# Shared values computed token by token, a shorter tail after attention, and two low parts moved to VectorE, in a two-layer RWKV and differential-attention trunk

## The reference, cut to what matters

```
x = x + (p @ w_up) * sigmoid(rmsnorm(x, g) @ w_gate)          # end of the first layer
h = rmsnorm(x, kv_norm_g)
k = rmsnorm_per_64(h @ w_k);  v = h @ w_v                      # v: 8 heads of 128
q = rmsnorm_per_64(rmsnorm(x, norm_g[1, 0]) @ w_q)
attn = softmax(q1 k1 + bias) - lam * softmax(q2 k2 + bias)     # per head, causal
o = rmsnorm_per_128(attn @ v) * (1 - lambda_init)
x = x + o @ w_o
x = x + squared_relu_mlp(rmsnorm(x, ...)) ; x = x + gated embedding
```

## Time and profile before

| what | us |
|---|---|
| three runs: median (lowest to highest) | 1518.47 (1514.57 to 1519.07) |
| the profiled execution: its own time | 1517.53 |
| its span in the profile | 1515.7 |
| TensorE busy, share of the span | 1451.2, 96% |
| DVE, ACT, POOL busy | 697.9, 583.2, 543.8 |

### The profile page before, as it was taken

The page is one execution under the profiler, slowest core; times in us unless marked ns, Lnnn a source line. Parts: engine busy times, 40 slices in busy tenths (PEclk is TensorE's granted clock), DMA queues, the critical chain, the costliest instruction groups (busy, mean ns, idle before and its releaser), DMA issues.

```text
span 1515.7 us, 23392 instructions
## 1 busy us (share of the span) xinstructions
PE 1451.2 (96%) x9087; PEld 1159.8 (77%) x9087; DVE 697.9 (46%) x1134; ACT 583.2 (38%) x922; POOL 543.8 (36%) x301
## 2 busy tenths in 40 slices
PE   6999998889999999999998999898999999999998
PEld 5767877756888888888876778565888888888877
DVE  7799977557443101331258323576453201331153
ACT  6785436454323111322244324385332211322252
POOL 3130013222443444343534334343334443444332
PEclk9999999999999999999999999899999999999999
DMA  6212100311323332323231522100132323222231
GB/s 192 83 56 84 56 1 10 114 31 39 100 85 109 111 97 83 111 83 111 87 108 65 167 84 83 56 2 29 56 106 88 112 97 111 84 95 99 95 99 56
DMA packets 121950, 126.45 MB, mean 83 GB/s; under 512 B 6268, under 2 KB 118652, under 8 KB 121864
## 3 DMA queue, kind: packets, MB, share of 16 engines
q1 hardware_dynamic: 121168, 123.99, 25.2%
q0 software_dynamic: 320, 0.66, 0.2%
q10 hardware_dynamic: 376, 0.61, 0.2%
HBM read 123.12 MB, written 2.12 MB: 83 GB/s over the span
## 4 chain that ended last, share of the span: by engine, by line
PE 84%; DVE 7%; ACT 4%; issue 3%; POOL 1%; ACTq 0%; DVEq 0%; POOLq 0%
PE pb L592 24%; PE pb L593 24%; PE pb L594 24%; ACT whi L1400 1%; PE pb L722 1%; PE pb L1306 1%; PE pb L1331 1%; PE pb L1315 1%; PE pb L797 1%; DVE xl L2363 1%; DVE Lg L2525 1%; DVE tmp L2447 1%; DVE At L2536 1%; POOL wlo L498 0%; PE pb L949 0%
## 5 line engine op out<-in xcount | busy, mean ns | idle before, releaser
L495 POOL TENSOR_TENSOR wlo<-wraw,whi 128x1024 fp32r<-128x1024 f32 x99 | 237.9, 2403 | 712.4 <-ACT whi L1400 698.7
L592 PE MATMUL pb<-xh,whi 128*128 128x512 f32 x1152 | 453.7, 394 | 6.2 <-DVE xl L2363 2.1
L593 PE MATMUL pb<-xl,whi 128*128 128x512 f32 x1152 | 448.6, 389 | 0.0
L594 PE MATMUL pb<-xh,wlo 128*128 128x512 f32 x1152 | 448.4, 389 | 0.0
L1400 ACT ACTIVATE whi<-wraw 128x2048 fp32r<-128x2048 f32 x108 | 206.2, 1909 | 225.1 <-PE pb L594 225.1
L592 PEld LDWEIGHTS pb<-xh,whi 128*128 128x128 f32 x1152 | 216.2, 188 | 67.3 <-issue 19.8
L594 PEld LDWEIGHTS pb<-xh,wlo 128*128 128x128 f32 x1152 | 216.3, 188 | 45.4
L593 PEld LDWEIGHTS pb<-xl,whi 128*128 128x128 f32 x1152 | 216.3, 188 | 44.4 <-issue 1.0
L498 POOL TENSOR_TENSOR wlo<-wraw,whi 128x1024 fp32r<-128x1024 f32 x99 | 243.9, 2464 | 0.0
L592 PE MATMUL pb<-hid_h,whi 128*128 128x512 f32 x512 | 199.3, 389 | 0.0
L594 PE MATMUL pb<-hid_h,wlo 128*128 128x512 f32 x512 | 199.2, 389 | 0.0
(11 more groups left out here) (306 smaller groups left out, 1685.7 us busy)
## 6 DMA issues: line engine op xcount, KB each, us to landing
wraw<-in_mlp_w_dram SPq DMA_DIRECT2D x128, 512.0 KB, 4.3
wraw<-in_rwkv_w_rkvo_dram SPq DMA_DIRECT2D x32, 512.0 KB, 4.4
wraw<-in_ple_w_gate_dram SPq DMA_DIRECT2D x16, 512.0 KB, 4.3
xtok<-in_x_dram SPq DMA_DIRECT2D x8, 512.0 KB, 6.3
wraw<-in_w_k_shared_dram SPq DMA_DIRECT2D x8, 512.0 KB, 4.0
wraw<-in_w_v_shared_dram SPq DMA_DIRECT2D x8, 512.0 KB, 4.3
wraw<-in_diff_w_q_dram SPq DMA_DIRECT2D x8, 512.0 KB, 3.9
wraw<-in_diff_w_o_dram SPq DMA_DIRECT2D x8, 512.0 KB, 4.3
```

Of the source, the lines that this page charges most:

```text
L495: pool.tensor_tensor(wlo[:, par, front], wraw[:, par, front], whi[:, par, front].bitcast(F32), ALU.subtract)
L592: mm(o, wh, ah, start=first, stop=False)
L593: mm(o, wh, al, start=False, stop=False)
L594: return mm(o, wl, ah, start=False, stop=last)
```

## The change

1. **Two low parts on VectorE.** wlo of blocks 58 and 59 is made by DVE (`slot_low`, one 128x2048 subtraction each) and not by POOL. In gate block b = 2 ACT makes whi of 58 ahead of the sigmoid, DVE makes its low part ahead of the products with UP, and chunk 0 of xh and xl of the key blocks is made there too.
2. **Values token by token.** `value_block` takes the activations as the stationary operand and 512 columns of the weights as the moving one, so V comes out with tokens on partitions: 4 token tiles t, 4 chunks k, 3 products, again 48 matmuls a block. The turns are gone. The norm's factor, which now differs by partition, is turned once (`rms_columns`, 4 transposes in block 59) and applied by ACT in the copy from PSUM (`v_take`, 8 times). DVE has no part in V. Weights of V are loaded in rows of 512 columns.
3. **First scores in the last query block.** Scores of step 0 stand in block 69, behind chunk 5, and their logits on DVE ahead of the last product with the norm. The reciprocal of norm group 3 is cut into four parts in steps 5 to 8 (`last_invert`); its spreads and products come one by one in steps 11 to 14. ACT's `high` of block 71 moves from step 10 to step 7.
4. **The output norm for six heads and for two.** `head_totals` comes for heads 0 to 3, 4 and 5 (at i = 32), and 6 and 7. Root and reciprocal of heads 0 to 5 are made while the last steps run; those of heads 6 and 7 go to other rows (`o_late`, 64 partitions), with the reciprocal behind DVE's product of head 3. The eight idle matmuls are gone. POOL makes xl of the attention output, after the low part of block 71, which now waits for the last `combine`.

```diff
@@ gpsimd
-            lows(L_MLP[0] + 33, N_KS + 2)
-
+            lows(L_MLP[0] + 33, N_KS)
+            pool.wait_ge(s.w_lo, N_KS + 2)
...
-            lows(N_DO + 1, N_DO + 3)
+            pool.wait_ge(s.at_rdy, 32)
+            low(N_DO + 1, 1, slice(0, 2048), False)
+            for h in range(8):
+                pool.wait_ge(s.x_hi, X_O + h + 1)
+                pool.tensor_tensor(xl[:, h, :], tmp[:, h % 4, :], xh[:, h, :].bitcast(F32), ALU.subtract).then_inc(s.x_ready, 1)
+            low(N_DO + 2, 0, slice(0, 2048), False)
@@ tensor
+            def value_block(j, hook):
+
+                n, par, hf = N_VS + j, (N_VS + j) % 2, j // 2
+                pe.wait_ge(s.w_lo, n + 1)
+                for t in range(TT):
+                    if j == 0 and t in (0, 2):
+                        pe.wait_ge(s.dense_v, 78 + t)
+                    elif j == 2:
+                        pe.wait_ge(s.v_ev, t + 1)
+                    for k in range(4):
+                        c, r = 4 * (j % 2) + k, slice(t * P, (t + 1) * P)
+                        (ah, al), w = xs(c), slice(512 * k, 512 * k + 512)
+                        mm(pb[t][:, :], ah[:, r], whi[:, par, w], start=c == 0, stop=False)
+                        mm(pb[t][:, :], al[:, r], whi[:, par, w], start=False, stop=False)
+                        ins = mm(pb[t][:, :], ah[:, r], wlo[:, par, w], start=False, stop=c == CT - 1)
...
+                if i == 32:
+                    head_totals((4, 5))
...
-            head_totals(1)
-            for j in range(8):
-                spin(j % 2, 384)
             pe.wait_ge(s.o_rs, 1)
-            for h in range(6):
+            pe.wait_ge(s.lg, 64)
+            pe.wait_ge(s.at_ev, 32)
+            for h in range(4):
                 head_rstd(h)
+            pe.wait_ge(s.o_rt, 1)
+            head_totals((6, 7))
+            head_rstd(4)
+            head_rstd(5)
...
-            proj(N_DO, X_O, 96, {1: last_rstd})
+            proj(N_DO, X_O, 88, {4: last_rstd})
@@ scalar
+                    if layer == 0 and b == 2:
+                        high(N_KS, N_KS % 2)
...
+            for k in range(4):
+                act.wait_ge(s.pe_step, 8 * (N_VS + 3))
+                query_high(k)
+            for t in range(TT):
+                v_take(1, t)
+            for k in range(4, CT):
+                act.wait_ge(s.pe_step, 8 * (N_VS + 4))
+                query_high(k)
...
+                if i == 33:
+                    act.wait_ge(s.o_ps, 2)
+                    A(rstd[:, :], pb[7][:, :], ACT.Sqrt, bias=eps_n, scale=1.0 / P).then_inc(s.o_rt, 1)
@@ vector
+                    if layer == 0 and b == 2:
+                        slot_low(N_KS)
...
                     if layer == 0 and b == 3:
                         splits(V_KV, X_KV, 6)
                         squares[0] += 2
+                        slot_low(N_KS + 1)
...
-                if i == 1:
-                    head_invert(3)
-                if i in (6, 7):
-                    head_norm(2 * i)
-                    head_norm(2 * i + 1)
+                if 5 <= i < 9:
+                    last_invert(i - 5)
+                if 11 <= i < 15:
+                    head_norm(i + 1)
...
+                if h >= 4:
+                    dve.wait_ge(s.x_ready, X_O + h - 3)
+                stt(tmp[:, h % 4, :], QT[:, h, :], subg, pb[O_BANK[h]][:, :], ALU.mult, ALU.mult).then_inc(s.o_f, 1)
+                if h == 3:
+                    dve.wait_ge(s.o_rt, 2)
+                    dve.reciprocal(o_late, o_late).then_inc(s.o_rs, 1)
```

More of the change, by code:

```diff
@@ L193, in trunk @@
         one_col = small[:, 184:217]
+        v_rms = small[:, 218:222]
         St = at("St", ST, [P, 5, CT, S])
@@ L461, in _ @@
                 sp.dma_start(strip[:, h, :], src).then_inc(s.strip_in, 16)
-            square(w_v_shared, N_VS)
+            wv = w_v_shared.rearrange("(k p) n -> p k n", p=P)
+            for j in range(4):
+                slot_free(N_VS + j)
+                par, k0, c0 = (N_VS + j) % 2, 4 * (j % 2), 512 * (j // 2)
+                for k in (0, 2):
+                    sp.dma_start(cols(wraw[:, par, :], 512, 4)[:, k:k + 2, :], wv[:, k0 + k:k0 + k + 2, c0:c0 + 512])\
+                        .then_inc(raw[par], 16)
             square(diff_w_q[0], N_Q)
@@ L1268, in f, with rms_columns @@
                             .then_inc(s.q_ps, 1)
                 return f
[L1271 to L1282, removed]
+            def rms_columns():
+                pe.wait_ge(s.dense_v, 74)
+                for t in range(TT):
+                    ins = pe.transpose(pb[7][:, t * P:(t + 1) * P], rstd[:, t * P:(t + 1) * P], ident)
+                ins.then_inc(s.vr_mm, 1)
@@ L1316, in attn_turn, with head_totals @@
                 ins.then_inc(s.at_tr, 1)
-            def head_totals(g):
-                pe.wait_ge(s.o_sq, 4 * g + 4)
-                for q in range(4):
-                    ins = mm(pb[7][32 * q:32 * q + 32, :], one_col[:, 1 - g:33 - g], tmp[:, q, :], start=(g == 0), stop=(g == 1))
+            def head_totals(heads):
+                pe.wait_ge(s.o_sq, heads[-1] + 1)
+                for h in heads:
+                    q, g = h % 4, h // 4
+                    ins = mm(pb[7][32 * q:32 * q + 32, :], one_col[:, 1 - g:33 - g], tmp[:, q, :],
+                             start=h not in (4, 5), stop=h not in (0, 1))
                 ins.then_inc(s.o_ps, 1)
@@ L2466, in head_invert, with last_invert @@
                 dve.reciprocal(head_rms[g][:, :], head_rms[g][:, :]).then_inc(s.qk_rs, 1)
+            def last_invert(t):
+                dve.wait_ge(s.qk_rt, 4)
+                part = head_rms[3][:, t * P:(t + 1) * P]
+                dve.reciprocal(part, part).then_inc(s.qk_rs, 1)
             def head_norm(i):
                 dve.wait_ge(s.q_ps, i + 1)
-                bank = pb[7 - i % 2 if i >= 12 else 4 + i % 4]
+                bank = pb[7 if i >= 12 else 4 + i % 4]
                 if i < 8:
@@ L2542, in invert_sums @@
                 dve.reciprocal(st_r[:, k:k + 2], st_l[:, k:k + 2]).then_inc(s.rec, 1)
+            for b in range(4):
+                if b == 3:
+                    head_invert(2)
+                    four_norms(2)
+                    dve.wait_ge(s.strip_in, 128)
+                    dve.wait_ge(s.pe_step, 8 * (N_Q + 3) + 4)
+                    logits(0)
+                times_rstd(N_Q + b, b, [head_tile(8 + 2 * b + m) for m in range(2)])
             dve.wait_ge(s.pe_step, 8 * N_DO)
-            dve.wait_ge(s.dense_v, 96)
+            dve.wait_ge(s.dense_v, 88)
             for i in range(32 + 3):
-                if i < 32:
+                if 0 < i < 32:
                     logits(i)
```

190 lines of the change are left out of this document (93 added, 97 removed).

## The result

| | us |
|---|---|
| kernel before, four runs: median (lowest to highest) | 1518.77 (1514.57 to 1519.29) |
| changed kernel, four runs: median (lowest to highest) | 1502.71 (1500.41 to 1504.81) |
| ratio, 95% interval | 0.99 (0.9887 to 0.9913) |
| the profiled execution: before, after | 1517.53, 1500.41 |
| its span: before, after | 1515.7, 1498.6 |

A forecast was written before the change was run, and what follows sets the result against it. TensorE was taken as the bound nearly everywhere. Gains of 4.5 + 2.8 + 1.3 + 6.7 = 15.3 us took the profiled 1517.53 us to 1502.2, said as 1502; its own range 1500 to 1506, with rivals 1496 to 1510.

The forecast's parts named there:

- low parts on VectorE: Blocks 58 and 59: DVE making the low parts removes TensorE's waits for xl; gain 4.5 us, bounds 2.1 to 5.
- V, net of `rms_columns`: Value blocks: four turns go, 3.2 us, four transposes give back 0.4; net gain 2.8 us.
- start of attention, scores included: First attention steps: shorter stall and cheaper spreads, less early scores' cost; gain 1.3 us, from loss 0.5 to gain 2.8.
- end of attention: Last difference to block 70: earlier root and reciprocal, less one half-clock loss; gain 6.7 us, bounds 4 to 8.5.
- the wait of 0.5 at chunk 4: Block 70: TensorE would wait about 0.5 us at chunk 4, after DVE's second reciprocal.
- One half-clock stretch: End of attention: pauses bring one stretch of some 3 us at half clock, costing 1.7 us.
- A: Both ends of attention: TensorE stays at full clock; gain 18.6 us, time 1499; chance 0.2.
- B: Clock lost longer or DVE late: chunk 6 stays late, block 67 waits; gain 7.4 us, time 1510; chance 0.2.
- C: Value blocks: activations as stationary operand expose their loading; at 0.1 us a matmul slower by 4 us, 1521; chance 0.03.
- D: Block 70: POOL paces chunks 1 to 7, not TensorE; at 2 us each, 4 us later, time 1506; chance 0.07.

The follow-up runs named there:

- run 1: Changed kernel with the low parts of blocks 58 and 59 back on POOL, new order kept; median 1507.64 us, ratio 0.9934.
- run 7: Changed kernel without POOL's wait for the last difference before the low part of block 71; median 1501.83 us, ratio 0.9902.
- run 5: Changed kernel, group 3's four lone spreads made two pairs: steps 8 and 14, median 1500.51 us; then steps 14 and 22, 1499.06 us.
- run 4: Changed kernel with the inverse sums of step 0 behind the logits of step 2 in DVE's queue; median 1501.52 us, ratio 0.989.
- run 6: Changed kernel with the root of heads 0 to 5 moved behind ACT's taking of the last head; median 1509.57 us, ratio 0.9943.
- run 8: Changed kernel plus idle matmuls before the turn of step 30 and before block 70, 1500.84 us; with only those before block 70, 1500.69 us.
- run 9: Changed kernel with ACT's xh of head 0 ahead of the root of heads 6 and 7; median 1500.53 us, ratio 0.9886.
- run 10: Changed kernel with step 0 scores behind block 69, paired spreads (steps 14, 22), xh first and both idle-matmul sets; median 1497.49 us, ratio 0.986.
- run 2: Changed kernel with 32 unused transposes, eight at a time, put into value blocks 64 and 65; median 1507.54 us, ratio 0.9937.

## Why the prediction was right, point by point

| term | forecast | measured, how |
|---|---|---|
| low parts on VectorE | 4.5 (2.1 to 5) | 5.4: first distance, 28.03 to 22.59 |
| V, net of `rms_columns` | 2.8 | 3.2: second distance 2.58, and 0.65 for the scores |
| start of attention, scores included | 1.3 (-0.5 to 2.8) | -0.1 (-0.5 to 0.5, see below): to step 28, 59.57 to 59.05, less 0.65 |
| end of attention | 6.7 (4 to 8.5) | 6.1: 9.51 from step 28 to the first spread, less 3.37 |
| sum | 15.3 | 14.7 |

That the sum is off by only 0.6 us is in part luck: the first two terms came 1.3 us above the forecast and the last two 2.0 below.

**Low parts.** The mechanism was right, shown by run 1: DVE is held up by POOL, and with POOL silent chunk 6 is there in time. One reading of the earlier trace rows was off: the product with UP ends at 816.12, 0.54 us behind POOL's instruction (815.58) and not with it, which is as if nearly all of it ran once POOL was done. Chunk 0's xl was due at 813.7 by the forecast, and comes at 810.87 in an execution that is 2.4 us ahead, at 813.3 on the clock of before. The gain was just above the upper bound: the waits removed were 2.07, 2.41 and 0.27, and a wait is counted from the modelled end of a matmul, 0.39 us behind its start, while the next could have begun 0.23 behind it, so that each hides 0.16 more. One part of the reasoning was not needed: the first of the two low parts does not pay at chunk 0, where the earlier order is enough; of the 5.4 us, run 1 gives 4.5 to the engine (3.4 without the clock's share) and the rest to the order.

The Trainium skill, SBUF — State Buffer, section Who interferes with whom, says that a VectorE instruction with two inputs in SBUF contends with a GpSimd instruction that reads SBUF, and that the ports they share are an exclusive lock. The traces agree: 2.87 or 2.88 us with POOL at work and 0.69 without, for the product with UP, and 2.82 against 0.75 for the difference (run 7).

**Values.** Right, and 0.4 more: a set of eight transposes costs 0.9 us, not the 0.79 from its start to the next one's. `rms_columns` gave back 0.4: 3.62 us saved over the value blocks, of which 3.23 (2.58 and 0.65) arrive at the end of block 69.

**Start of attention.** This is the term of the sum that was mis-sized, by 1.4 us; the mechanism stood. The forecast put the four lone spreads at 2.1 us, half of the 1.06 that two of them take in the earlier trace rows. But those two ran side by side on different rows of the array. One alone takes 1.06 just as well, and four side by side too (857.05 to 858.12), in the changed kernel's timeline of TensorE among the key blocks:

```profile
857.05 1.14 PE L1276 MATMUL pb<-head_rms,cst 32*128 32x512 f32 x8
858.12 0.50 PE L605 MATMUL pb<-xh,whi 128*128 128x512 f32 x1
```

Cutting the group of spreads into four single ones thus doubles their time on TensorE to 4.2 us, of which 3.9 show in the steps (run 5): 1.8 more than counted. Something that the forecast did not mention gave 1.05 of them back. In the kernel before, ACT makes the high part of block 71 in step 10, from 993.10 for 1.90 us, and the next turn waits for ACT's copy behind it:

```profile
995.52 0.63 PE L1315 MATMUL pb<-cst,At 128*128 128x128 f32 x4 [1.02 <-ACT ATt L1917]
```

The change moves this high part to step 7. So the stretch from step 11 to step 12 takes 3.38 us before, with that wait, and 3.37 after, with the first lone spread. From step 11 to step 28 it is 33.10 us before and 36.11 after, 3.0 lost where 2.1 were counted. Up to step 11, ahead of all four, the lead was 3.5 us where the forecast's own numbers make 3.9; and the early scores cost 0.65, not 0.5. The rest of that part came as said: TensorE resumed after 2.59 us (forecast 2.5), because of the inverse sums in DVE's queue, and run 4 shows that even without them nothing would be won. The half clock lasted 6.8 us, from 965 to 972, where before it was over 10.

The term depends on that clock. In three other profiles (run 6 and both of run 8) the half clock lasts 3.4 us there, in the rest 6.8, and step 28 comes 58.45 to 59.42 us behind block 69 in the eight profiles that have the changed kernel's program up to it. Against the one profile of before this is -0.5 to 0.5 us, still below the 1.3.

**End of attention.** The first spread came 9.5 us earlier, as forecast. From there to block 70 it took 5.0 us, not 4.2: ACT's root of two heads was put at 0.3 us and takes 0.7 (1032.87 to 1033.58), some 0.3 behind the first product, since it waits for TensorE's sum of squares. Run 9 shows that it stood in the way: with xh first, block 70 starts 0.9 earlier. Of the 9.5 us ahead of the first spread, run 6 gives 5.2 to the early root and run 7 1.6 to POOL's wait; the remaining 2.7, the idle matmuls among them, have no run of their own. On the other side, the wait of 0.5 at chunk 4 did not come. One half-clock stretch, 3.4 us long, came and lay wholly in block 70: eight starts 0.43 apart instead of 0.23 are 1.6 us, forecast 1.7. That it came once and no longer decides between the forecast and rivals A and B, and it was no certainty: six of the twelve other profiles show full clock all through the tail, three with idle matmuls and three without.

The Trainium skill, TensorE: Matmul & The Clock Gate, section What's actually happening, has the low clock as the default, released by activity. The traces agree on the direction: the root made late (run 6) leaves TensorE idle for 6.56 us ahead of the first spread and comes with 17 us of half clock. That the removed idle matmuls had kept the clock up for block 70 stays open: with such matmuls and without, block 70 was seen at full clock.

**Rivals.** A (no clock lost) is what runs 5, 8, 9 and 10 show in the tail; none shows it at the start of attention. B did not come: chunk 6 was in time and block 67 waited for nothing. C is excluded by run 2. D: POOL takes 1.25 us a chunk (4.99 for four), and TensorE waits for it only at the start, and for 0.3 us more in run 9; block 70 is not paced by it.

## What to carry to other kernels

Before a group of small matmuls is cut up and spread over a pipeline, look whether they ran side by side: if one costs as much as four, spreading them multiplies the price, and only what falls into existing waits is free: here four lone ones took 4.2 us where two pairs take 2.1, and 3.9 of the 4.2 stood in the steps. When an elementwise operation on VectorE is four times as long as its twin elsewhere, look at what GpSimd does at that moment; moving the GpSimd work can be worth more than any reordering. A stall at the start of a pipeline is the length of a chain: taking one instruction out of the way moves the wait to the next link, so that the whole chain must be walked before the gain is counted.

## What the runs showed of the hardware that was not expected

- A spread of 32 rows by 512 columns takes TensorE 1.06 us alone, two on different rows take 1.06, four take 1.07, all at full clock.
- DVE's reciprocal takes 3.35 us for 128 partitions of 512, and 3.35 for 64 partitions: half the partitions save nothing. A quarter of the columns takes 0.95 us.
- After eight transposes the next 512-column matmul holds its successor back by 0.32 us, not 0.23.
- Half clock was seen while TensorE was in use by small matmuls: at 0.50 it was busy 5.42 of 6.00 us at the start of attention.
